# Second matmul of each indexer score: 64 rows of the array instead of 128

## The chip, the cores and the metric

The kernel runs on one core of one Trainium2 chip. The metric is the device time of one execution in microseconds (us); less is better. Before the change it was measured three times.

## The reference

One layer of a hybrid decoder block over 512 tokens of width 1024: a combined input projection, three attention branches (A sparse, B differential, C dilated), gates, an output projection, and a SwiGLU feed-forward part. The part that matters here is branch A's indexer, which scores each visible key for each query and keeps the 128 best:

```python
score = einsum('bqh,bqhs->bqs', wi, relu(einsum('bqhd,bsd->bqhs', qi, k_idx)))
score = where(key_pos <= q_pos, score, -inf)
_, sel = top_k(score, topk)      # 8 index heads, 64 dims each, topk 128
```

Queries come in four blocks of 128. In the first block every visible key is kept, so only blocks 1 to 3 are scored, with 256, 384 and 512 keys. That makes 8 heads x 3 blocks = 24 score tiles of 128 queries by 256, 384 or 512 keys.

## The kernel before

One program per engine, written out by hand; semaphores order them. TensorE's program (from L736) is a long sequence of projections. A projection multiplies float32 values as two rounded parts each, hi and lo (type float32r), in three matmuls for each block of 128 input channels: hi x hi (L756), lo x hi (L757), hi x lo (L758), added up in a PSUM bank. ScalarE makes the hi part of each weight chunk (L1135), VectorE the lo part (L1422), and SyncE loads the chunks.

Order on TensorE around the change: transposes and the projection of the input's first chunks (L756 to L758), a values projection (L772 to L774), four transposes of the normalised latent (L829), then the indexer's 24 pairs (L834 to L845), and behind them a loop of six projections for branch C (L847 to L849), then attention.

The indexer's operands:

- `iq_split` [128, 8, 512]: per head h, 64 partitions hold the hi part of the query and the other 64 its lo part. The hi part lies in partitions 0 to 63 for even heads and 64 to 127 for odd ones (L1174, L1175); VectorE writes the lo part into the other half (L1478 to L1480).
- `ik_hi` and `ik_lo` [128, 512]: the hi and the lo part of the keys, each written twice, into both halves of the partitions (L1185, L1186, L1488, L1489).

So a matmul over all 128 partitions with `ik_hi` gives (q_hi + q_lo) k_hi, and one with `ik_lo` gives (q_hi + q_lo) k_lo. Both go into one bank, the second adding to the first. Tile n = 3 h + i - 1 (head h, block i) uses bank n modulo 4 of `s_ps[0], s_ps[1], t_ps[0], t_ps[1]`.

Each tile runs through three engines: TensorE's pair (`idx_made`), ScalarE's relu out of the bank (L1209, `idx_relu`), and VectorE's weighted accumulation into `score` (L1517, `idx_added`). TensorE's pair n waits for relu n - 4 (L839), relu n for accumulation n - 4 (L1208), and accumulation n for accumulation n - 3 (L1516). Tile 2 also waits for `kv_ready`, VectorE's copy of `kv_T` out of the bank that the tile takes (L837). The score tiles then go to VectorE's search for the largest (L1533, L1541), in parts between the making of the lo chunks.

Other matmuls in the kernel use 64 partitions of the array: the scores of branch C (L883, L888) and of branch B (L897), and the latent queries (L955), in plain float32. The trace counts two records for each plain float32 matmul.

Of the kernel before, what the change touches and what calls it, by code (L numbers as in the profile page):

```python
# [22 lines left out]
P = 128  # L23
# [4 lines left out]
DH = 64  # L28
# [164 lines left out]
def hybrid_block(nc, a, out):  # L193
# [3 lines left out]
    def place(name, at_kb, shape, dt=F32):  # L197

        return nc.alloc_sbuf_tensor_at(name, shape, dt, offset=16512 + int(at_kb * 1024))

    def sem(name):
        return ctx.enter_context(nc.semaphore(name))

    with ctx:
# [30 lines left out]
        iq_split = place("iq_split", R + 103, [P, 8, S], F32R)  # L235
        ik_hi = place("ik_hi", R + 17, [P, S], F32R)
        ik_lo = place("ik_lo", R + 19, [P, S], F32R)
# [149 lines left out]
        idx_made = sem("idx_made")  # L387
# [348 lines left out]
        def _(pe):  # L736
# [59 lines left out]
            for j in range(3):  # L796
                pe.matmul([t_ps[0], t_ps[1], s_ps[1]][j][0:24, :], relb[:, :], onehot[:, j * S:(j + 1) * S],
                          start=True, stop=True).then_inc(pe0, 1)
# [34 lines left out]
            wait_tile_out(pe, 3)  # L833
            for n in range(24):  # L834
                h, i = n // 3, n % 3 + 1
                if n == 2:
                    pe.wait_ge(kv_ready, 1)  # L837
                if n >= 4:
                    pe.wait_ge(idx_relu, n - 3)  # L839
                ps = [s_ps[0], s_ps[1], t_ps[0], t_ps[1]][n % 4]  # L840

                pe.matmul(ps[:, 0:P * (i + 1)], iq_split[:, h, i * P:(i + 1) * P],
                          ik_hi[:, 0:P * (i + 1)], start=True, stop=False)
                pe.matmul(ps[:, 0:P * (i + 1)], iq_split[:, h, i * P:(i + 1) * P],
                          ik_lo[:, 0:P * (i + 1)], start=False, stop=True).then_inc(idx_made, 1)  # L845

            with pe.Fori(0, 3) as i:  # L847
                for j in range(2):
# [1058 lines left out]
```

## Time and profile before

| | |
|---|---|
| median of 3 runs | 1067.65 us |
| lowest, highest | 1062.47, 1073.39 us |
| the profiled execution | 1067.65 us |
| its span, first to last instruction | 1065.7 us |
| TensorE matmul records | 1000.4 us (94% of the span) |
| VectorE, ScalarE, GpSimd busy | 483.5, 412.5, 115.2 us |
| mean granted TensorE clock | 0.979 of full speed |

Matmuls are pipelined, so a record reaches from its start to its modelled end and overlaps the next one; the distance between starts is what a matmul costs. PEld is the weight load that belongs to a matmul. A load that starts while the matmul before it still streams is hidden; where a load starts together with its own matmul's record, it isn't.

### The profile page before, as it was taken

The page shows a single profiled execution, that of the slowest core. Times are in us where ns is not written, and L with a number is a line of the kernel's source. Part 1 is how long each engine was busy: PE and PEld are TensorE (multiplying, and loading weights), DVE is VectorE, ACT ScalarE, POOL GpSimd, SP SyncE. Part 2 cuts the span into 40 slices and gives each one's busy share as a digit, 9 for nine tenths or more (in the row PEclk, how much of TensorE's full clock was granted, in tenths as well). Part 3 has the DMA queues.
Part 4 walks back from the last instruction along what each step waited for, and adds up shares of the span by engine and source line. Part 5 has one row for each costly group of instructions (what it writes and reads, how often), then busy time and mean ns, then how long its engine had stood idle before and what let it go on. Part 6 is the DMA issues. An engine that isn't in the chain of part 4 may idle for free.

```text
span 1065.7 us, 12662 instructions
## 1 busy us (share of the span) xinstructions
PE 1000.4 (94%) x4831; PEld 807.7 (76%) x4831; DVE 483.5 (45%) x803; ACT 412.5 (39%) x676; POOL 115.2 (11%) x136
## 2 busy tenths in 40 slices
PE   2389999999999999999999999799999999999997
PEld 0367878878877676777888888588888888788886
DVE  3372497853335335545546368532323333322331
ACT  4243343245555555642222222343335343412231
POOL 3100000000035331200000007400000000001111
PEclk9689999999999999999999999899999999999999
DMA  8942222621132201043565692123232323223312
GB/s 311 365 132 89 79 80 79 176 81 40 47 106 68 60 22 40 30 146 115 186 202 181 211 330 80 40 79 118 82 115 79 101 96 117 70 79 109 104 35 79
DMA packets 93262, 121.49 MB, mean 114 GB/s; under 512 B 4680, under 2 KB 83109, under 8 KB 93090
## 3 DMA queue, kind: packets, MB, share of 16 engines
q1 hardware_dynamic: 92690, 114.67, 32.6%
q0 software_dynamic: 528, 6.22, 1.9%
q8 instruction: 29, 0.48, 0.2%
q14 instruction: 15, 0.12, 0.0%
HBM read 118.20 MB, written 8.45 MB: 119 GB/s over the span
## 4 chain that ended last, share of the span: by engine, by line
PE 88%; DVE 3%; DMA 3%; ACT 2%; SPq 2%; issue 1%; POOL 0%; POOLq 0%; DVEq 0%; ACTq 0%
PE tile_ps L756 24%; PE tile_ps L758 24%; PE tile_ps L757 24%; DMA w_raw<-in_w_in_dram 3%; PE s_ps L894 2%; PE o_ps L941 2%; PE t_ps L912 2%; SPq L512 2%; PE s_ps L897 1%; PE tile_ps L955 1%; PE tile_ps L1000 1%; PE tile_ps L961 1%; PE tile_ps L1001 1%; PE tile_ps L1002 1%; DVE w_lo L1422 1%
## 5 line engine op out<-in xcount | busy, mean ns | idle before, releaser
L756 PE MATMUL tile_ps<-h_hi,w_hi 128*128 128x512 f32 x816 | 326.6, 400 | 24.1 <-DVE h_lo L1462 16.4
L757 PE MATMUL tile_ps<-h_lo,w_hi 128*128 128x512 f32 x816 | 319.8, 392 | 0.0
L758 PE MATMUL tile_ps<-h_hi,w_lo 128*128 128x512 f32 x816 | 319.7, 392 | 0.0
L1422 DVE TENSOR_TENSOR w_lo<-w_raw,w_hi 128x2048 fp32r<-128x2048 f32 (+2 forms) x78 | 172.3, 2209 | 259.3 <-ACT w_hi L1135 259.2
L756 PEld LDWEIGHTS tile_ps<-h_hi,w_hi 128*128 128x128 f32 x816 | 153.9, 189 | 69.2 <-issue 28.9
L1135 ACT ACTIVATE w_hi<-w_raw 128x2048 fp32r<-128x2048 f32 (+2 forms) x78 | 143.8, 1844 | 95.2 <-PE tile_ps L758 68.5
L758 PEld LDWEIGHTS tile_ps<-h_hi,w_lo 128*128 128x128 f32 x816 | 153.9, 189 | 33.5
L757 PEld LDWEIGHTS tile_ps<-h_lo,w_hi 128*128 128x128 f32 x816 | 154.2, 189 | 30.4
L756 PE MATMUL tile_ps<-f_hi,w_hi 128*128 128x512 f32 x176 | 69.2, 393 | 2.5 <-DVE f_lo L1838 2.5
L758 PE MATMUL tile_ps<-f_hi,w_lo 128*128 128x512 f32 x176 | 69.0, 392 | 0.0
L757 PE MATMUL tile_ps<-f_lo,w_hi 128*128 128x512 f32 x176 | 69.0, 392 | 0.0
L1250 ACT ACTIVATE nl<-nl,cst 128x256 f32<-128x256 f32 (+3 forms) x81 | 43.0, 532 | 55.4 <-DVE cst L1585 55.3
L1385 ACT ACTIVATE f_hi<-f_t 128x512 f32 x22 | 13.9, 633 | 95.5 <-DVE f_t L1834 95.5
L716 POOL TENSOR_TENSOR sq_acc<-x 128x512 f32<-128x512 f32 x2 | 2.1, 1041 | 442.0 <-DVE x L1848 267.4
L687 POOL TENSOR_TENSOR tm<-tab,score 128x256 f32<-128x256 f32 (+2 forms) x24 | 24.4, 1015 | 185.8 <-DVE cst L1585 185.8
L1834 DVE TENSOR_TENSOR f_t<-tile_ps,silu_t 128x512 f32<-128x512 f32 x22 | 15.2, 692 | 60.2 <-PE tile_ps L758 60.2
L1262 ACT ACTIVATE pt<-t_ps 128x128 f32<-128x128 f32 (+2 forms) x80 | 32.1, 402 | 26.8 <-PE t_ps L912 26.2
L756 PEld LDWEIGHTS tile_ps<-f_hi,w_hi 128*128 128x128 f32 x176 | 33.4, 190 | 9.9 <-DVE f_lo L1838 2.9
L757 PEld LDWEIGHTS tile_ps<-f_lo,w_hi 128*128 128x128 f32 x176 | 33.4, 190 | 7.0
L758 PEld LDWEIGHTS tile_ps<-f_hi,w_lo 128*128 128x128 f32 x176 | 33.3, 189 | 6.9
L1380 ACT ACTIVATE silu_t<-tile_ps 128x512 f32<-128x512 f32 x22 | 13.2, 600 | 46.3 <-PE tile_ps L758 46.1
L1585 DVE CUSTOM_DVE_ANT_0 nl<-s_ps,tm 128x256 f32<-128x256 f32 (+2 forms) x24 | 13.4, 557 | 36.6 <-PE s_ps L894 36.4
(272 smaller groups left out, 1350.7 us busy)
## 6 DMA issues: line engine op xcount, KB each, us to landing
w_raw<-in_w_in_dram SPq DMA_DIRECT2D x31, 1024.0 KB, 5.3
w_raw<-in_w_gate_up_dram SPq DMA_DIRECT2D x22, 1024.0 KB, 5.1
ada<-in_w_ada_dram SPq DMA_DIRECT2D x16, 1024.0 KB, 5.9
ada<-in_w_ada_dram SPq DMA_DIRECT2D x16, 512.0 KB, 14.4
w_raw<-in_w_down_dram SPq DMA_DIRECT2D x8, 1024.0 KB, 5.3
row_copies<-row_flat POOLq DMA_DIRECT2D x1, 5632.0 KB, 23.4
w_raw<-in_w_out_dram SPq DMA_DIRECT2D x4, 1024.0 KB, 9.5
tab<-row_copies SPq DMA_DIRECT2D x12, 256.0 KB, 2.6
```

Source lines behind the costliest of these rows:

```text
L512: sp.dma_start(ada1[g][k][:], a["w_ada"][0][k * P:(k + 1) * P, g * D:(g + 1) * D]) \
L687: pool.tensor_tensor(tm[v % 2][:, 0:w], table_of(v), score[:, off:off + w], ALU.add) \
L756: pe.matmul(tile_ps[b][0:mw, :], wh, x_hi[:, kx, :], start=start, stop=False)
L757: pe.matmul(tile_ps[b][0:mw, :], wh, x_lo[:, kx, :], start=False, stop=False)
L758: mm = pe.matmul(tile_ps[b][0:mw, :], wl, x_hi[:, kx, :], start=False, stop=stop)
L894: mm = pe.matmul(ps[:, 0:w], qlat[h % 2][:, i * P:(i + 1) * P], kv_T[:, 0:w], start=True, stop=True)
L912: mm = pe.transpose(t_ps[v % 2][:, j * P:(j + 1) * P], src[:, j * P:(j + 1) * P], ident[:])
L941: mm = pe.matmul(o[:, i * P:(i + 1) * P], kv_nat[:, j, :], p_j, **flags)
L1135: nc.scalar.activation(w_hi[s][:, 0:kt, :], w_raw[s][:, 0:kt, :], ACT.Copy).then_inc(w_hi_made[s], 1)
L1250: act.activation(b, b, ACT.Exp, bias=negmax[:, k:k + 1], scale=-1.0, accum_out=expsum[:, k:k + 1]).then_inc(exped, 1)
L1262: act.activation(pt[v % 2][:, 0:w], t_ps[v % 2][:, 0:w], ACT.Copy).then_inc(pt_ready, 1)
L1422: dve.tensor_tensor(w_lo[s][:, 0:kt, :], w_raw[s][:, 0:kt, :], w_hi[s][:, 0:kt, :].bitcast(F32), ALU.subtract) \
```

## The change

The second matmul of each pair reads 64 partitions of both operands instead of 128, those that hold the hi part of the query (`d0` is 0 for even heads, 64 for odd ones). It computes q_hi k_lo in place of (q_hi + q_lo) k_lo; the product q_lo k_lo is no longer added. The first matmul, the bank, the order and all waits stay.

```diff
             for n in range(24):
                 h, i = n // 3, n % 3 + 1
+                d0 = DH * (h % 2)
                 if n == 2:
                     pe.wait_ge(kv_ready, 1)
                 if n >= 4:
@@
                 pe.matmul(ps[:, 0:P * (i + 1)], iq_split[:, h, i * P:(i + 1) * P],
                           ik_hi[:, 0:P * (i + 1)], start=True, stop=False)
-                pe.matmul(ps[:, 0:P * (i + 1)], iq_split[:, h, i * P:(i + 1) * P],
-                          ik_lo[:, 0:P * (i + 1)], start=False, stop=True).then_inc(idx_made, 1)
+                pe.matmul(ps[:, 0:P * (i + 1)], iq_split[d0:d0 + DH, h, i * P:(i + 1) * P],
+                          ik_lo[d0:d0 + DH, 0:P * (i + 1)], start=False, stop=True).then_inc(idx_made, 1)
```

## Rows read from the trace of the kernel before

**Rows 1.** The page: span, busy time of each engine, the chain that ended last.
```profile
span 1065.7 us, 12662 instructions
...
PE 1000.4 (94%) x4831; PEld 807.7 (76%) x4831; DVE 483.5 (45%) x803; ACT 412.5 (39%) x676; POOL 115.2 (11%) x136
...
PE 88%; DVE 3%; DMA 3%; ACT 2%; SPq 2%; issue 1%; POOL 0%; POOLq 0%; DVEq 0%; ACTq 0%
```

**Rows 2.** Windows: length, busy (records) of PE, PEld, DVE, ACT, POOL, clock, DMA share, GB/s.
```profile
127.00:138.50 11.50, 11.31 (x55) 7.68 (x54) 10.46 (x20) 10.13 (x22) 0.00 (x0) 1.00 0.00 0
```

**Rows 3.** Timeline of the indexer stage: start, duration (us), engine, line, operation.
```profile
127.29 0.19 PEld L842 LDWEIGHTS s_ps<-ik_hi,iq_split 128*128 128x128 f32 x1
...
128.34 0.19 PEld L842 LDWEIGHTS t_ps<-ik_hi,iq_split 128*128 128x128 f32 x1 [0.51 <-DVE kv_T L1506]
...
130.42 11.21 DVE L1517 SCALAR_TENSOR_TENSOR score<-relu_t,cst,score 128x256 f32<-128x256 f32 x21
...
133.12 0.19 PEld L842 LDWEIGHTS t_ps<-ik_hi,iq_split 128*128 128x128 f32 x1 [0.20 <-ACT relu_t L1209]
133.12 0.50 PE L842 MATMUL t_ps<-ik_hi,iq_split 128*128 128x512 f32 x1
...
133.76 0.19 PEld L842 LDWEIGHTS t_ps<-ik_hi,iq_split 128*128 128x128 f32 x1 [0.34 <-ACT relu_t L1209]
...
138.24 0.19 PEld L756 LDWEIGHTS tile_ps<-h_hi,w_hi 128*128 128x128 f32 x1
138.47 0.39 PE L756 MATMUL tile_ps<-h_hi,w_hi 128*128 128x512 f32 x1
```

**Rows 4.** Timeline, TensorE's matmuls in the same stage where no wait stands between.
```profile
129.73 0.40 PE L844 MATMUL s_ps<-ik_lo,iq_split 128*128 128x512 f32 x1
129.96 0.28 PE L842 MATMUL t_ps<-ik_hi,iq_split 128*128 128x256 f32 x1
130.08 0.28 PE L844 MATMUL t_ps<-ik_lo,iq_split 128*128 128x256 f32 x1
130.20 0.34 PE L842 MATMUL t_ps<-ik_hi,iq_split 128*128 128x384 f32 x1
130.37 0.34 PE L844 MATMUL t_ps<-ik_lo,iq_split 128*128 128x384 f32 x1
```

**Rows 5.** Waits, 127 to 138.6 us: us in total, times, longest.
```profile
PEld s_ps L842 <- ACT relu_t L1209: 1.5, 7, 0.3
```

**Rows 6.** Groups by form: busy us, mean ns of one record, idle before.
```profile
L955 PE MATMUL tile_ps<-aq_T,w_uk_sb 64*128 64x512 f32 x16 | 9.0, 641 | 1.0 <-DVE oc_lo L1594 1.0
...
L894 PE MATMUL s_ps<-kv_T,qlat 128*128 128x512 f32 x16 | 8.2, 597 | 0.0
```

**Rows 7.** Timeline around a 64-row group (L883) between 128-row matmuls.
```profile
230.24 0.40 PE L757 MATMUL tile_ps<-h_lo,w_hi 128*128 128x512 f32 x1
230.47 0.40 PE L758 MATMUL tile_ps<-h_hi,w_lo 128*128 128x512 f32 x1
...
230.80 0.30 PEld L883 LDWEIGHTS s_ps<-cqk 64*128 64x128 f32 x4 [0.37 <-issue]
...
231.22 0.50 PE L756 MATMUL tile_ps<-h_hi,w_hi 128*128 128x512 f32 x1
231.56 0.40 PE L757 MATMUL tile_ps<-h_lo,w_hi 128*128 128x512 f32 x1
```

**Rows 8.** Timeline, two 64-row groups (L897), the second with what follows.
```profile
408.01 0.70 PE L897 MATMUL s_ps<-bqk 64*128 64x256 f32 x2 [1.20 <-DVE cst L1585]
...
418.23 1.13 PE L897 MATMUL s_ps<-bqk 64*128 64x512 f32 x4
419.29 0.50 PE L756 MATMUL tile_ps<-h_hi,w_hi 128*128 128x512 f32 x1
```

**Rows 9.** Windows around a fall of the granted clock (columns of rows 2).
```profile
405.50:408.90 3.40, 2.00 (x11) 1.07 (x8) 2.69 (x5) 0.91 (x4) 0.77 (x1) 1.00 0.05 3
408.90:412.30 3.40, 2.90 (x7) 2.32 (x8) 1.61 (x7) 1.54 (x5) 0.45 (x1) 0.50 0.48 154
```

## The prediction

> **What bounds the kernel now.** I read the page first [rows 1]: TensorE's matmul records cover 1000.4 of the 1065.7 us, and 88% of the chain that ended last is TensorE. Outside a few stages nothing but TensorE's own sequence sets the end, so whatever makes TensorE reach a later instruction late moves the end by as much, unless a later wait soaks it up. The run that was profiled took 1067.65 us, 2 us outside its span, and is itself the median of the three runs shown, so a change of the span is added to 1067.65.
>
> The changed lines are the indexer's 24 pairs of matmuls (L842, L844), so the next view is the table of windows for that stage [rows 2]: TensorE is busy for 11.31 of 11.50 us, ScalarE for 10.13, VectorE for 10.46. All three look full. The timeline tells which one paces [rows 3]. VectorE's 21 accumulations run without a gap from 130.42 for 11.21 us, 0.534 us each. TensorE's pairs do have gaps: the pair with 512 columns at 133.12 starts after 0.20 us of waiting for a relu, and the next pair 0.64 us later. Where no wait stands between, a matmul follows the one before after 0.12 us (256 columns), 0.17 us (384) or 0.23 us (512) [rows 4], so a pair needs 0.24, 0.35 or 0.46 us, 0.35 on average, against the 0.53 that VectorE grants. The waits view confirms the direction: the weight loads of L842 wait for the relus, twelve times in all, seven of them in the row shown [rows 5]. So here TensorE has slack of 0.18 us a pair, and only here; behind the stage stands its dense stream again.
>
> The stage as TensorE sees it begins with the load at 127.29 and ends where L756's first matmul starts, at 138.47 [rows 3].
>
> **The change, part by part.** The first matmul of a pair stays as it is, 128 rows of the array. The second uses 64 rows, at partition 0 for even heads and 64 for odd ones. Nothing else is added: 48 matmuls and 48 weight loads before and after, the same columns, the same waits, no DMA, nothing queued anew. One product is left out, that of the two low parts.
>
> *What half the rows save.* A matmul's time could depend on its rows. The forms view has 64x512 matmuls (L955) at a mean of 641 ns and 128x512 ones (L894) at 597 [rows 6]: fewer rows are no faster. I cost the saving at 0. Were the second matmul free, the gain would still be small: the pairs wait for VectorE anyway, and only the last pair stands on the path, with 0.23 us. That is the bound on the gain.
>
> *What the alternation adds.* The trace has no pair of the new kind (the rounded type, 64 rows), but it has other 64-row matmuls between 128-row ones. Into 64 rows: L757 starts at 230.24 and L758 at 230.47, the usual 0.23. The load for the 64-row L883 starts at 230.80, 0.33 after L758, when that matmul is nearly out of the array, instead of while it streams [rows 7]. So the switch waits for the end: 0.10 us. Then the load is not hidden either. Back to 128 rows: L756's matmul record begins together with its load (231.22) and lasts 0.50 instead of 0.40, and L757 follows after 0.34 instead of 0.23, so an exposed load is 0.11 us [rows 7]. I take the same 0.10 for the wait before it. A group checks the sum: two 64-row matmuls of 512 columns at L897 (four records) start at 418.23 and the next 128-row matmul at 419.29, 1.06 us [rows 8]. If the two heads run side by side, on their own halves of the array, each streams 4 passes of 512 columns at the full clock of 2.4 GHz, 0.85 us; load and drain are the other 0.21. One switch therefore costs 0.21 us.
>
> Each pair now holds two switches, into the half array and back: 0.42 us. A pair takes 0.24 + 0.42 = 0.66 us at 256 columns, 0.77 at 384 and 0.88 at 512, on average 0.77. That is more than the 0.53 us of VectorE, so the slack of 0.18 us is used up and TensorE paces the stage. Eight pairs of each width: 8 x (0.66 + 0.77 + 0.88) = 18.5 us. From 127.29 this gives 145.8 for L756's load, whose own exposure brings its matmul to 145.9, where it was 138.47: 7.4 us late. The wait of the third pair for kv_T, which held its load until 128.34 [rows 3], is covered: two pairs of 0.66 and 0.77 reach 128.72. The ring of four banks doesn't bind, since ScalarE and VectorE need 0.5 us a piece and are now the ones that wait.
>
> Bounds of a switch: nothing below, since the new form isn't in the trace; 0.10 if only the drain is paid and the load hidden, which makes a pair 0.55, 13.2 us for 24, and 2.3 us on the path; 0.21 at the rows; 0.25 if the rounding form drains more slowly, for 9.3 us. I take 0.21, because both 64-row groups shown give it, one of 128 columns a head and one of 512 [rows 7, 8].
>
> On this the Trainium skill has a rule, "TensorEngine Tiling (Array Packing)", section "Key Properties": changing the tiling mode, not just the tile, drains TensorE. It names no price; by it the 0.10 us before the load at 230.80 is paid at all 48 switches, and this trace's rows agree; left to the rows alone the sum is the same.
>
> *What is late next.* VectorE and ScalarE leave the stage some 6 us later, TensorE 7.4. Nothing there catches up or falls behind: TensorE then has 48 dense matmuls (11 us at 0.23) from a chunk split before; the next chunk's lo part follows the last accumulation on VectorE and takes 2.2 us there. On the page of the profile only 3% of the chain that ended last is DMA [rows 1], which a late TensorE could soak up; the rest of the chain hangs on TensorE's own results. So the 7.4 us reach the end: 1067.65 + 7.4 = 1075.0.
>
> **The rivals.** *A, not slower: the switch hides.* The mechanism is the slack of 0.18 us in each pair: as long as a switch costs under 0.09 us, VectorE goes on pacing and only the last pair is longer. Up to there the time is 1067.7, 0.2 at the most below it and up to 0.2 above; at 0.10 it is 1070. For it: the wait before each pair is real, and the new matmul accumulates into the same bank with the same stationary block. Against it: the load at 230.80 [rows 7] had nothing else to wait for and did not go early, while L756's at 138.24, between matmuls of one shape, goes 0.23 us ahead of its matmul [rows 3]. The Trainium skill gives this rival a rule too, "TensorE: Matmul & The Clock Gate", section "Step-by-step: what each phase is for": loads are pulled ahead of matmuls in flight when the rows don't conflict or the background weight buffer takes them. By it the half load would hide and the time stay at 1067.7; the 230.80 row disagrees.
>
> *B, the clock falls.* Streaming is 24 pairs x 0.35 = 8.4 us, 77% of the stage now and 46% of 18.5 us after. The granted clock fell to half at 408.9, after a stretch in which TensorE was busy for 2.00 of 3.40 us [rows 9]. If it fell for the whole stage, streaming would double: 8.4 us more, 1083.4. For a part of it, in proportion. Against it: in that stretch TensorE stood still for 1.20 us on VectorE [rows 8]; here the longest pause would be a drain and a load, 0.21 us.
>
> *C, the new form has a price of its own*, say a second pass for 64 rows: 24 x 0.175 = 4.2 us more, 1079. Nothing in the trace speaks for it.
>
> **How the numbers follow.** Chances: 0.68 for the forecast, 0.17 for A with its intermediate prices, 0.10 for B, 0.05 for C and others. The predicted time is 1075.0. Its own range is 1073 to 1077, from switches of 0.18 to 0.25 us. The three runs of before lie between 1062.47 and 1073.39, so measurement alone moves a median by some 3 us. The range of 8 in 10 reaches down to A (1068), since A is too likely to leave out, and up to 1082, which covers C and most of B. A change of over 1%, 10.7 us, is about what a measurement can tell from none. The forecast lies at 0.7%: I give 0.15 of its chance to over 1% by scatter, and to that B and a third of C, together 0.22 for slower. Faster is left with 0.02, as no mechanism gives more than 0.2 us. Same: 0.76.
>
> **What would show it.** In the changed profile: L844's loads start together with their matmul records, which are some 0.10 us longer, and 0.33 us (at 512 columns) after L842's start; L842's loads likewise behind L844; pairs 0.66, 0.77 and 0.88 us apart with no wait for relu; VectorE's accumulations with gaps of some 0.24 us before them, waiting for ScalarE, that for L844; L756 starting near 145.9; a granted clock of 1.00 in the stage; and from there on every row later by 7.4 us. I am wrong if the loads of L844 stay hidden (A), if the stage ends near 138.5, if the clock drops in it (B), or if a later wait shrinks by what the stage has grown.

## The result and the profile after

The changed kernel takes 1084.30 us (median of 4 runs, 1081.64 to 1088.15), the kernel before beside it 1069.02. The ratio is 1.0147 with a 95% interval of 1.0100 to 1.0195. In a later comparison with 6 runs of it against 17 it was 1.0178 (1.0140 to 1.0217). The change makes the kernel slower by some 1.5%, where 0.7% was forecast. The profiled execution has a span of 1083.3 us against 1065.7, so 17.6 us have to be found.

The page of the changed kernel answers to [rows 1]: the chain is as much TensorE's as before, and the line of the clock in 40 slices shows where it is new. PEclk (second fence) has a 5 in the sixth slice, 135 to 162 us, where the kernel before had a 9.

```profile
span 1083.3 us, 12662 instructions
...
PE 1019.8 (94%) x4831; PEld 816.7 (75%) x4831; DVE 485.5 (45%) x803; ACT 413.2 (38%) x676; POOL 115.1 (11%) x136
...
PE 89%; DMA 3%; DVE 2%; ACT 2%; SPq 2%; issue 1%; POOL 0%; POOLq 0%; DVEq 0%; ACTq 0%
```

```profile
PEclk9689959999999999999999999899999999999999
```

The timeline of TensorE in the changed kernel's indexer stage (start, duration in us, engine, line; the changed lines are L843 and L845 there) answers to [rows 3, 4]:

```profile
127.05 0.36 PE L843 MATMUL s_ps<-ik_hi,iq_split 128*128 128x256 f32 x1
127.34 0.38 PE L845 MATMUL s_ps<-ik_lo,iq_split 64*128 64x256 f32 x1
127.65 0.44 PE L843 MATMUL s_ps<-ik_hi,iq_split 128*128 128x384 f32 x1
...
128.39 0.50 PE L843 MATMUL t_ps<-ik_hi,iq_split 128*128 128x512 f32 x1
128.82 0.50 PE L845 MATMUL t_ps<-ik_lo,iq_split 64*128 64x512 f32 x1
129.25 0.38 PE L843 MATMUL t_ps<-ik_hi,iq_split 128*128 128x256 f32 x1
...
131.88 0.58 PE L843 MATMUL t_ps<-ik_hi,iq_split 128*128 128x256 f32 x1
...
134.14 0.79 PE L843 MATMUL s_ps<-ik_hi,iq_split 128*128 128x512 f32 x1
134.86 0.79 PE L845 MATMUL s_ps<-ik_lo,iq_split 64*128 64x512 f32 x1
135.59 0.58 PE L843 MATMUL s_ps<-ik_hi,iq_split 128*128 128x256 f32 x1
...
154.09 0.79 PE L756 MATMUL tile_ps<-h_hi,w_hi 128*128 128x512 f32 x1
...
158.09 0.44 PE L756 MATMUL tile_ps<-h_hi,w_hi 128*128 128x512 f32 x1
```

The first rows are the forecast's: three pairs (256, 384, 512 columns) take 0.60, 0.74 and 0.86 us, together 2.20 (127.05 to 129.25), where 0.66, 0.77 and 0.88 were worked out. Then the same three pairs take 3.71 us (131.88 to 135.59). The weight loads show what lies between (columns as above):

```profile
128.39 0.19 PEld L843 LDWEIGHTS t_ps<-ik_hi,iq_split 128*128 128x128 f32 x1 [0.19 <-issue]
128.82 0.18 PEld L845 LDWEIGHTS t_ps<-ik_lo,iq_split 64*128 64x128 f32 x1 [0.25 <-issue]
...
131.16 0.28 PEld L845 LDWEIGHTS s_ps<-ik_lo,iq_split 64*128 64x128 f32 x1 [0.36 <-issue]
```

Each of the 48 loads starts together with its own matmul, to 0.03 us, so none is hidden, and from 131 us on a load lasts 0.28 us in place of 0.18. The windows (columns of [rows 2]) give the clock:

```profile
127.05:130.80 3.75, 3.75 (x14) 2.00 (x12) 2.60 (x5) 2.16 (x6) 0.00 (x0) 1.00 0.00 0
130.80:154.10 23.30, 23.30 (x39) 10.60 (x38) 12.09 (x20) 9.24 (x19) 0.00 (x0) 0.50 0.00 1
154.10:158.10 4.00, 4.00 (x11) 3.13 (x11) 2.23 (x2) 2.40 (x2) 0.00 (x0) 0.50 0.00 0
158.10:160.00 1.90, 1.90 (x10) 1.56 (x9) 1.90 (x5) 0.00 (x0) 0.00 (x0) 0.99 0.00 0
```

The granted clock falls to 1.2 GHz 3.75 us after the first pair and comes back at 158.1, 4 us into the dense matmuls. TensorE's records leave no gap in all that time.

The account, from the first pair's start (127.32 before, 127.05 after) to the first dense matmul (138.47 and 154.09): 11.15 us before and 27.04 after, 15.9 more. Eight times 2.20 is 17.6 us, what the stage would last at full clock: 6.5 us are the switches. The other 9.4 us are the clock's. Behind the stage nine dense matmuls take 4.00 us (154.09 to 158.09) in place of 2.07 at 0.23, 1.9 us more. Sum 17.8, less 0.27 for the earlier start: 17.5 of the 17.6 us. Nothing else moved: the first matmul of the transposes in attention (L912, now L913) starts at 251.8 in place of 234.1, and the end comes later by the same amount.

The waits view of the changed kernel, from 127 us to the end of the stage, shows who now waits for whom: VectorE for ScalarE, and ScalarE for TensorE. Of the twelve waits of TensorE's loads for a relu one is left, of 0.2 us. It answers to [rows 5]:

```profile
DVE score L1518 <- ACT relu_t L1210: 11.4, 15, 0.9
ACT relu_t L1210 <- PE s_ps L845: 7.8, 12, 1.0
```

### The profile page after: what moved, and what is told of

Read it like the earlier page. It is cut to its first block, busy times and chain, and to the rows that moved or that the text cites. A ratio compares the mean times of both kernels' runs of the same rounds, so it can differ in the third digit from the quotient of the medians.

```text
span 1083.3 us, 12662 instructions
## 1 busy us (share of the span) xinstructions
PE 1019.8 (94%) x4831; PEld 816.7 (75%) x4831; DVE 485.5 (45%) x803; ACT 413.2 (38%) x676; POOL 115.1 (11%) x136
## 4 chain that ended last, share of the span: by engine, by line
PE 89%; DMA 3%; DVE 2%; ACT 2%; SPq 2%; issue 1%; POOL 0%; POOLq 0%; DVEq 0%; ACTq 0%
PE tile_ps L756 24%; PE tile_ps L758 24%; PE tile_ps L757 23%; DMA w_raw<-in_w_in_dram 3%; PE s_ps L895 2%; PE t_ps L913 2%; PE o_ps L942 2%; SPq L512 1%; PE s_ps L898 1%; PE tile_ps L956 1%; PE tile_ps L1001 1%; PE tile_ps L962 1%; PE tile_ps L1002 1%; PE tile_ps L1003 1%; PE t_ps L843 1%
## 5 line engine op out<-in xcount | busy, mean ns | idle before, releaser
L1263 ACT ACTIVATE pt<-t_ps 128x128 f32<-128x128 f32 (+2 forms) x80 | 32.0, 401 | 27.1 <-PE t_ps L913 26.4
```

The source lines that it names most:

```text
L1263: act.activation(pt[v % 2][:, 0:w], t_ps[v % 2][:, 0:w], ACT.Copy).then_inc(pt_ready, 1)
```

## The experiments

Two questions: is the price that of the switch between 128 and 64 rows, and what lowered the clock? "Pace" below is the mean time from pair to pair, from three or six of them. Stage lengths run from the first pair to the first dense matmul behind it.

**Both matmuls on 64 rows: no switch inside the stage.**

```diff
-                pe.matmul(ps[:, 0:P * (i + 1)], iq_split[:, h, i * P:(i + 1) * P],
-                          ik_hi[:, 0:P * (i + 1)], start=True, stop=False)
+                pe.matmul(ps[:, 0:P * (i + 1)], iq_split[d0:d0 + DH, h, i * P:(i + 1) * P],
+                          ik_hi[d0:d0 + DH, 0:P * (i + 1)], start=True, stop=False)
```

> The changed kernel, but with 64 rows in the first matmul of each pair too (it leaves out q_lo k_hi), so that no switch between 128 and 64 rows is left inside the stage, only at its two ends. Theory (the switch's wait and open load cost 0.21 us each, and the clock fell because the switches left TensorE's array unfed half of the time): pairs 0.24, 0.35 and 0.46 us long again, VectorE paces the stage at 0.53 us a pair, TensorE is through the stage in 11 to 11.5 us, granted clock 1.00 in it, time within 0.3% of before. Rival (fewer rows in the array are what lowers the clock, or the 64-row form is slow by itself): a clock of 0.5 in the stage again or pairs over 0.6 us, stage of 15 us or more, time 0.4 to 1.5% over before.

Measured: ratio 1.0024 (0.9991 to 1.0057), so no loss is shown; stage 11.7 us. Both sides were half right. The timeline shows 64-row matmuls at or near the old distances (0.12 us behind one of 256 columns, 0.18 behind one of 384), so the form itself has no price:

```profile
136.07 0.28 PE L845 MATMUL s_ps<-ik_lo,iq_split 64*128 64x256 f32 x1
136.19 0.38 PE L843 MATMUL t_ps<-ik_hi,iq_split 64*128 64x384 f32 x1
136.41 0.33 PE L845 MATMUL t_ps<-ik_lo,iq_split 64*128 64x384 f32 x1
136.59 0.42 PE L843 MATMUL t_ps<-ik_hi,iq_split 64*128 64x512 f32 x1
136.85 0.39 PE L845 MATMUL t_ps<-ik_lo,iq_split 64*128 64x512 f32 x1
```

But the clock fell, without a single switch between the pairs (windows, columns of [rows 2]):

```profile
132.40:138.50 6.10, 5.99 (x31) 4.00 (x30) 5.52 (x10) 5.25 (x13) 0.00 (x0) 1.00 0.00 0
138.50:144.10 5.60, 5.60 (x20) 4.73 (x18) 5.60 (x12) 5.17 (x12) 0.00 (x0) 0.50 0.00 0
144.10:148.70 4.60, 4.60 (x12) 3.63 (x12) 4.33 (x6) 2.65 (x3) 0.00 (x0) 0.50 0.01 4
```

At the same pace, set by VectorE, the kernel before kept 1.00 with 128-row pairs [rows 2]: its fifteenth pair starts 5.80 us after the first, that of this kernel 5.63 us. The profiled run is the slowest of the ten, but the fall isn't its alone: the mean granted clock of the ten runs has a median of 0.974, that of the kernel before beside them 0.979, which is some 10 us more at half clock, as long as the fall in the profile.

The stage hides the slow clock here. Three pairs still take 1.59 us at half clock (139.29 to 140.88), VectorE's pace, though doubled distances would make them 2.1 us. One reason is that 64-row matmuls of two heads, which lie on different halves of the array, partly run side by side: L843 of the next head starts at 140.28, ahead of the second matmul of the head before it, at 140.38. Only the dense matmuls behind the stage pay.

**Half as many switches.** In odd tiles the 64-row matmul comes first (the lines that these replace are left out).

```diff
+                full = (iq_split[:, h, i * P:(i + 1) * P], ik_hi[:, 0:P * (i + 1)])
+                part = (iq_split[d0:d0 + DH, h, i * P:(i + 1) * P], ik_lo[d0:d0 + DH, 0:P * (i + 1)])
+                first, second = (full, part) if n % 2 == 0 else (part, full)
+                pe.matmul(ps[:, 0:P * (i + 1)], *first, start=True, stop=False)
+                pe.matmul(ps[:, 0:P * (i + 1)], *second, start=False, stop=True).then_inc(idx_made, 1)
```

> The changed kernel with the two matmuls of every odd tile swapped (64 rows first), so that 64-row matmuls stand in twos and 128-row ones in twos: 24 switches in place of 48, same work, same waits. Theory: a pair costs 0.35 + 0.21 = 0.56 us on average, just over VectorE's 0.53; stage of 13.5 to 14.5 us, 2.5 to 3 us more than before; streaming share 62%, clock stays at 1.00; time +0.2 to 0.4%. If the clock falls nonetheless: +1% or more. Rival (the price hangs on the number of 64-row matmuls, not of switches): pairs of 0.77 us, clock 0.5 and +1.4% as in the changed kernel.

Measured: ratio 1.0030 (0.9996 to 1.0063), as forecast, though its interval just reaches no change at all. The 64-row matmuls and the products are the changed kernel's, only their order differs. The stage lasted 12.8 us, less than forecast: six pairs take 3.16 us (134.50 to 137.66 in its timeline), 0.53 a pair, which is 0.35 + 0.18 and VectorE's pace at once. A part of what it is under the forecast comes from four places where two 64-row matmuls of different heads meet and start together, which the forecast left out; the one of 256 columns, 0.12 us, is then hidden. The rows at one of them, and the clock, which stayed:

```profile
131.67 0.49 PE L847 MATMUL t_ps<-ik_lo,iq_split 64*128 64x512 f32 x1
131.67 0.38 PE L846 MATMUL t_ps<-ik_lo,iq_split 64*128 64x256 f32 x1
```

```profile
130.20:143.00 12.80, 12.80 (x52) 6.95 (x51) 11.96 (x22) 10.60 (x24) 0.00 (x0) 1.00 0.00 1
```

So the price hangs on the number of switches, not on that of the 64-row matmuls.

**All 48 switches, with dense matmuls between.** The 48 matmuls of the next projection are issued two behind each pair, and the loop of projections behind the stage begins with its second. Of the edit the part that places them is shown; the wait for the chunk, the signal at the projection's end and the shortened loop are left out.

```diff
+                m, kt = n // 12, n % 12
+                fb = tile_start(TL_CQK + m) if kt == 0 else (TL_CQK + m) % 2
+                for q in (2 * kt, 2 * kt + 1):
+                    k, part_ = divmod(q, 3)
+                    wk = (w_lo if part_ == 2 else w_hi)[fs][:, k, m * P:(m + 1) * P]
+                    xk = (h_lo if part_ == 1 else h_hi)[:, k, :]
+                    mm = pe.matmul(tile_ps[fb][:], wk, xk, start=q == 0, stop=q == 23)
```

> The changed kernel with all its 48 switches, but the 48 matmuls of the projection that follows (L756 to L758, 128 rows, 512 columns) moved into the stage, two behind each pair. Theory of two terms: the switches cost what they cost (24 x 0.42 us), so a pair with its two fillers takes 0.77 + 0.46 = 1.23 us, 29.5 us in all; before, stage and projection took 11.2 + 10.9 = 22.1 us, so +7.4 us or +0.7%; the array is fed 66% of the time and the clock stays at 1.00, which gives back the 8 us that the changed kernel lost to the clock: about 8 us less than the changed kernel. Rival (64-row matmuls or switches lower the clock whatever stands between): clock 0.5 in the stage, 1.6 to 2% over before.

Measured: ratio 1.0109 (1.0050 to 1.0167; 4 runs). Stage and projection took 28.5 us with the clock at 1.00, but behind them TensorE stood still for 4.15 us for the next chunk's lo part, which VectorE makes only after its last accumulation. The clock fell 0.5 us before that pause ended, for 3.4 us:

```profile
131.80:160.20 28.40, 28.40 (x97) 15.68 (x95) 14.78 (x24) 11.38 (x24) 0.00 (x0) 1.00 0.00 1
...
165.00:170.00 5.00, 4.92 (x16) 4.00 (x17) 5.00 (x19) 0.47 (x1) 0.00 (x0) 0.70 0.67 210
```

So two causes were mixed, and a second kernel splits the chunk in the middle of the stage (shown is VectorE's part; ScalarE makes the chunk's hi part behind relu 11 in the same way):

```diff
                     .then_inc(idx_added, 1)
+                if n == 11:
+                    make_lo(CH_CQK + 1)
```

> The filled kernel again (48 switches, two dense matmuls behind each pair), with the next weight chunk's hi and lo part made in the middle of the stage instead of behind it, so that TensorE need not wait 4 us for them at its end. Theory of two terms (switches 0.42 us a pair, the rest of the changed kernel's loss is the clock): stage and projection together 28.5 us, as the first filled kernel had them, against 22.1 before: +6.4 us, +0.6%; clock 1.00 all through, no wait of TensorE behind it. Rival (switches lower the clock themselves, only later): clock 0.5 somewhere from the stage to 170 us, over +1%.

Measured: ratio 1.0088 (1.0059 to 1.0116), 1075.90 us. The stage with its projection lasted 29.8 us (123.16 to 152.94), which holds 0.8 us of waiting for a bank at its end; before they took 11.15 + 10.9 = 22.1. That is 7.7 us or 0.72%, inside the interval, and 6.9 us without the wait. The changed kernel's loss at full clock is thus there by itself. The mean granted clocks of its ten runs, 0.974 to 0.984, lie clear of the changed kernel's 0.962 to 0.971; a shorter fall in some of them they can't exclude. The profile's clock:

```profile
128.00:152.90 24.90, 24.34 (x81) 13.18 (x79) 14.54 (x22) 12.13 (x23) 0.00 (x0) 1.00 0.14 43
```

**The first matmul alone**, no 64 rows and no switch.

```diff
-                          ik_hi[:, 0:P * (i + 1)], start=True, stop=False)
-                pe.matmul(ps[:, 0:P * (i + 1)], iq_split[:, h, i * P:(i + 1) * P],
-                          ik_lo[:, 0:P * (i + 1)], start=False, stop=True).then_inc(idx_made, 1)
+                          ik_hi[:, 0:P * (i + 1)], start=True, stop=True).then_inc(idx_made, 1)
```

> The kernel before without the second matmul of each pair (it leaves out q k_lo): no 64-row matmul, no switch, half the streaming. VectorE goes on pacing at 0.53 us a tile and TensorE streams 0.175 us of it, 33%. Theory that the clock falls with the share of time in which the array is fed: granted clock 0.5 from some 4 us into the stage until the dense matmuls behind it have run a few us; the stage stays at 11 us, as 0.35 us at half clock still fits into 0.53; time +1 to +4 us, from the dense matmuls that run slow at its end. Rival (the switch itself lowers the clock): clock 1.00 all through, time equal to before or 0.2 us less.

Measured: ratio 1.0000 (0.9964 to 1.0036). The clock fell, though 7.7 us into the stage and not 4, and stayed low until 146.8, 3.6 us behind it. The loss that this should bring, 2 us at most, can't be told from none.

```profile
132.30:140.00 7.70, 6.53 (x21) 3.10 (x19) 7.13 (x14) 6.90 (x16) 0.00 (x0) 1.00 0.00 0
140.00:143.20 3.20, 3.11 (x6) 1.99 (x7) 3.20 (x8) 2.97 (x7) 0.00 (x0) 0.50 0.00 0
```

So switches aren't needed for a fall, nor 64-row matmuls. One 128-row matmul for each 0.53 us did not keep the clock, two did. In this stage TensorE did pause, 1.2 us in all before the fall, 0.5 us at the longest.

**128-row pairs at the changed kernel's pace.** Extra relus into unused memory slow ScalarE down; TensorE's pairs are those of the kernel before.

```diff
+                for q in range(1 if n < 20 else 0):
+                    f0 = 200 * (n + q)
+                    act.activation(cqk.rearrange("p a s -> p (a s)")[:, f0:f0 + 200],
+                                   [s_ps[0], s_ps[1], t_ps[0], t_ps[1]][n % 4][:, 0:200], ACT.Relu)
```

> The kernel before (pairs of two 128-row matmuls, no switch) with a 200-column relu into unused memory ahead of each of the first 20 relus, so that ScalarE paces the tiles at about 0.8 us, near the 0.77 us that the changed kernel's switches gave at full clock. TensorE is fed 0.35 of 0.8 us, the same share of time as in the changed kernel, but with all 128 rows. If the share of time alone lowers the clock: 0.5 in the stage as in the changed kernel, time +0.9 to +1.2%. If 64-row matmuls count for less than 128-row ones (as in the kernel with both on 64 rows, whose clock fell at VectorE's old pace): clock 1.00 in the stage, +7 us, +0.6 to 0.7%.

Measured: ratio 1.0011 (0.9984 to 1.0038). It missed its aim: the pace was 0.62 us (three pairs from 131.62 to 133.47), 0.09 over VectorE's 0.53 and not 0.27. The rows of ScalarE (relus of 256, 200 and 384 columns) show why. By their ends, 130.96, 131.19 and 131.58, the further relu takes 0.23 us and the next one of the kernel 0.39; those of 256 and 512 columns take 0.28 and 0.49. So ScalarE needed 0.39 us a tile by itself, and 0.15 us of what was added went into its slack against VectorE:

```profile
130.41 0.55 ACT L1213 ACTIVATE relu_t<-s_ps 128x256 f32<-128x256 f32 x1
130.67 0.52 ACT L1211 ACTIVATE cqk<-t_ps 128x200 f32<-128x200 f32 x1
130.89 0.69 ACT L1213 ACTIVATE relu_t<-t_ps 128x384 f32<-128x384 f32 x1
```

The clock stayed at 1.00, which at this pace decides nothing.

The second kernel of the kind puts three relus of 66 columns in place of the one:

> As the kernel with a relu of 200 columns, but with three relus of 66 columns ahead of each of the first 20 relus, for a pace of about 1.1 us a tile with 128-row pairs and no switch. Either theory of how TensorE is fed gives a clock of 0.5 from some 4 us into the stage until the dense matmuls have run again, and +1.6 to +1.8% (13 us from the pace, 3 to 5 from the slow dense matmuls). Only a theory in which the switch itself lowers the clock gives 1.00, and +1.2%.

Measured: ratio 1.0047 (1.0017 to 1.0076). Here too the pace fell short of what was meant, 1.1 us. It came to 0.74 us, the mean from 129.94 to 134.37 over six pairs:

```profile
129.94 0.50 PE L842 MATMUL t_ps<-ik_hi,iq_split 128*128 128x512 f32 x1
...
134.37 0.50 PE L842 MATMUL s_ps<-ik_hi,iq_split 128*128 128x512 f32 x1
```

That is the changed kernel's pace at full clock, 0.73 us. TensorE streams the same columns for the same part of the time in both; only the rows of the second matmul, and what fills the rest (waiting here, drains and open loads there), differ. Here the clock stayed:

```profile
124.00:139.40 15.40, 13.06 (x47) 6.82 (x46) 12.14 (x22) 15.40 (x83) 0.00 (x0) 1.00 0.00 0
```

Its expectation, a fall whatever the theory and at least 1.2%, was missed; it was written for the slower pace and can't be held against this one. The loss of 4.7 us agrees with the stage's 15.9 us (123.47 to 139.37) against 11.15.

**The changed kernel again, beside the others.**

> The changed kernel once more, on the chip of the other runs, for comparison with them. If its loss has two terms, the switches (stage 18.5 us in place of 11.2 at full clock) and the clock (half from some 4 us into the stage until dense matmuls have run a few us behind it, 8 to 9 us), it is 1.3 to 1.6% over before, and 6 to 8 us over the filled kernel whose clock stayed up (+0.88%). If the fall of the clock in its profile was chance, most runs are at +0.7%.

Measured: ratio 1.0178 (1.0140 to 1.0217), 1086.48 us. Stage 27.1 us (129.50 to 156.57), clock at half from 133.3, 3.8 us into it, to 160.6. The lowest of its 6 runs is 1080.99, 15 us over the other kernel's median, so the fall in the profile was not chance. The mean granted clock says the same: 0.962 to 0.971 in all 13 runs of the changed kernel, 0.973 to 0.982 in the runs of the kernel before. The changed kernel lies 0.9%, 9.6 us by the ratios, over the filled kernel with the same 48 switches. By the account above the clock costs 9.4 + 1.9 = 11.3 us, and the filled kernel has 0.8 us of waiting of its own.

**A version meant to beat both**: 128-row pairs, two dense matmuls behind each, so that TensorE never waits for VectorE. The edit is that of the filled kernel, chunk split in the middle included, made on the kernel before. A first form:

> The kernel before with both matmuls on 128 rows, no switch, and the 48 dense matmuls of the next projection placed two behind each pair (chunk split in the middle of the stage). TensorE then never waits for VectorE's 0.53 us: 24 x (0.35 + 0.46) = 19.4 us in place of 22.1. Theory: 2.7 us less, -0.25%, clock 1.00 in the stage. Rival: VectorE and ScalarE, which now also make a chunk in the middle, become the pace and nothing is won, within 0.1% of before.

Measured: ratio 1.0002 (0.9977 to 1.0027). Stage and projection 20.5 us, of which 0.8 us is a wait for a bank, [0.80 <-ACT cqk L1151] in its timeline. The second form copies that tile out behind relu 14 (and no longer behind the stage):

```diff
                     make_hi(CH_CQK + 1, TL_CQK - 1)
+                if n == 14:
+                    evacuate(TL_CQK, cqk[:, 0, :], -ATTN_SCALE)
```

> The interleaved kernel with 128-row pairs, with the first projection tile copied out in the middle of the stage instead of behind it, so that the wait of 0.8 us for its bank goes. Stage and projection 19.5 us in place of 22.1: 2.6 us less than before, -0.25%; its interval may still touch 0. If it isn't under before by the profile's stage either, the interleaving doesn't pay.

Measured: ratio 0.9990 (0.9963 to 1.0017). The stage and projection are 19.5 us (124.86 to 144.39) in place of 22.1, as worked out, but 2.5 us of 1066 can't be told from none. It isn't shown to be faster than the kernel before; it is clearly faster than the changed one.

These two also give the price of the switches by itself, since the filled kernel with the early chunk differs from the first of them only in the rows of each second matmul, and all three keep the clock in the stage. Without the waits at the end, stage and projection take 29.0 us with 48 switches and 19.5 without: 9.5 us, or 0.20 a switch. The times agree: 1.0088 against 1.0002 is 9.2 us, and the stages of those two, each with its wait, differ by 9.3.

## Why the prediction was wrong

- *VectorE paces the stage before, slack 0.18 us a pair*: right. With half the switches a pair costs 0.35 + 0.18 us, and the stage grew by only 1.6 us.
- *Fewer rows save nothing*: right for the changed kernel, whose 64-row matmuls stand alone. In the kernel with both on 64 rows they have the 128-row distances, except where two on different halves of the array meet and run side by side.
- *A switch waits for the matmul ahead and leaves the load open, 0.21 us*: right, slightly too dear. 17.6 us instead of 18.5 for 24 pairs gives (17.6 - 8.4) / 48 = 0.19 us, and the filled kernel against the interleaved one 0.20. No load hid, which answers rival A. One sign was put down wrong: L844's load was to come 0.33 us after L842's start at 512 columns. That leaves out L842's own open load; 0.44 belongs to the forecast's pair of 0.88, and 0.43 was measured (128.39 to 128.82). The rule of the Trainium skill quoted in the prediction, that changing the tiling mode drains TensorE ("TensorEngine Tiling (Array Packing)", section "Key Properties"), agrees with the trace at every pair.
- *TensorE takes over as the pace, +7.4 us to the end*: right as a term, 6.5 us by the profile and 0.6 to 1.2% in the filled kernel, where it stands alone.
- *No later wait soaks it up*: right, 17.5 of 17.6 us are accounted for by the stage and the 4 us behind it.
- *The granted clock stays at 1.00*: wrong, and this is the step that failed. The clock was argued from one row of the kernel before [rows 9], whose fall followed a pause of 1.20 us [rows 8], and I took the pause for the reason: here the longest would be 0.21 us. No row showed that a fall needs a pause. The changed kernel's clock fell after 3.75 us of gapless records. Rival B was written out, with 10% for it, and it is what happened.
- *B's price, 8.4 us*: too low. It doubled only the streaming. At half clock the drains and the loads last longer too: 3.71 against 2.20 us for three pairs is 0.50 us a pair, where the doubled streaming would be 0.35. The dense matmuls up to the return of the clock cost 1.9 us more, which the price had left out. Since not the whole stage ran slow, the sum is 11.3 us.
- *The share of streaming* (77% before and 46% after in the prediction; 8.4 us of 11.2 and of 18.5 are 75% and 45%) took no account of the rows. The kernel with both on 64 rows ran its pairs at the old pace and lost the clock; the one with 128-row pairs at 0.74 us kept it. So 64-row pairs lost the clock at a pace at which 128-row pairs kept it. What differs there is the rows, and what comes with them: the product left out, and up to the fall two places where matmuls of two heads overlap. The changed kernel lost it at 0.73 us, where 128-row pairs kept it at 0.74; there the drains and open loads differ as well, and how much they add to the rows' part was not tried and stays open.

With the fall known, 1067.65 + 6.5 + 11.3 = 1085.5 us, against 1084.30 and 1086.48 measured. The terms come from the changed kernel's own profile, so this closes the account and doesn't test it; the tests are the filled and the interleaved kernels.

## What to carry to other kernels

Cutting rows off a single matmul saved no time here, and where it alternates with full-height ones each change costs a drain and an open load, 0.19 to 0.20 us; if such matmuls must be, put those of one height next to one another, which took the same work from +1.5% to +0.3%, hardly to be told from none. A gapless row of TensorE records is no sign that the clock will hold: look at what fills them, and price a fall with everything TensorE does in the stage and a few us behind it. A stage in which another engine sets the pace is where such a fall hides first.

## What the runs showed of the hardware

- The clock fell with alternating heights (3.75 us into the stage, in records without a gap), with 64-row pairs (6.1 us in, 0.1 us of gaps), and with one 128-row matmul per 0.53 us (7.7 us in, 1.2 us of gaps). It held with 128-row pairs at 0.53, 0.62 and 0.74 us, with alternating heights in twos at 0.53 us, and with two dense matmuls behind each alternating pair.
- At 1.2 GHz not only streaming is slower: a weight load's record went from 0.18 to 0.28 us, a 512-column pair with two switches from 0.86 to 1.45 us.
- Two 64-row matmuls on different halves of the array run side by side: those of 512 and 256 columns at 131.67 above, and the next 128-row one starts 0.42 us later, as behind the one of 512 columns alone.
- ScalarE's relus out of PSUM overlap one another: one of 200 columns has a record of 0.52 us and adds 0.23 us from end to end.
- The first pair of the stage starts anywhere from 123.16 to 132.43 us in the profiles, though nothing ahead of it differs between the kernels. It goes with how long TensorE's clock is at half before 85 us: about 20.5 us in the five profiles whose stage starts at 123.16 to 124.86, and about 30.7 us in the four at 129.50 to 132.43. In a late one the clock was at half up to about 67 us, against 57 in an early one. Whole runs fit: of the kernel before, those with a mean clock of 0.982 have spans of 1059.7 to 1062.5 us, and those at 0.974 or less 1069.8 to 1073.6. So most of the scatter goes with the clock, and effects under 0.3% could not be told here; why the early stretch varies was not looked into. The windows show it, the early kernel (one further relu) first, then the late one (both on 64 rows):

```profile
56.00:60.00 4.00, 3.93 (x16) 2.66 (x15) 3.60 (x7) 1.90 (x3) 0.00 (x0) 0.93 1.08 302
```

```profile
60.00:66.00 6.00, 3.93 (x9) 3.13 (x10) 5.76 (x11) 3.45 (x6) 0.00 (x0) 0.50 0.57 138
```
